# Cached index keys transposed during the opening, the sample indexer spread over the first late projection units, and attention's high halves made by GpSimd

## What is computed

```python
xn = rms_norm(x, norm1_g) * (1 + sc1) + sh1          # sc1, sh1 from silu(c) @ w_ada + b_ada
qa, ka, va, qb, kb, vb, iq, ik, iw = split_proj(xn @ w_in)
...
def indexer_scores(iq, iw, ik):                      # 8 heads of width 64
    dots = jnp.einsum('nqhd,nld->nqhl', iq, ik) * IDX_DIM ** -0.5
    return jnp.einsum('nqh,nqhl->nql', iw, jax.nn.relu(dots))
...
# sample: the index keys of the past come from paged memory
ik_all = concatenate([cache_idx_k[page_table].reshape(N, past, IDX_DIM), ik], axis=1)
sel, ok = select_keys(indexer_scores(iq, iw, ik_all), qpos, topk)
...
# mixer A (8 heads): three dilated windows, merged; mixer B (8 query heads, 2 key heads):
# softmax over the keys that the indexer chose
o = concatenate([oa, ob]); x = x + g1 * (o @ w_out)
x = x + g2 * ((silu(gate) * up) @ w_down)            # gate, up = xn2 @ w_gate_up
```

## Time and profile before

| what | value |
| --- | --- |
| device time, median of 3 runs (lowest to highest) | 1853.21 us (1852.08 to 1859.09) |
| profiled execution: its time, and its span | 1854.12 us, 1852.0 us |
| busy: PE, DVE, ACT, POOL | 1639.8, 872.8, 699.8, 551.4 us (89, 47, 38, 30% of the span) |
| HBM read, written | 115.29 MB, 27.04 MB (77 GB/s over the span) |

### The profile page before, as it was taken

How to read it: one execution, slowest core, us unless ns; L and a number is a source line. 1 busy time by engine, 2 the same in 40 slices (tenths; PEclk the granted TensorE clock), 3 DMA queues, 4 the chain that set the end, 5 groups by cost and what they waited for, 6 DMA issues and landing times.

```text
span 1852.0 us, 29649 instructions
## 1 busy us (share of the span) xinstructions
PE 1639.8 (89%) x10770; PEld 1520.8 (82%) x10770; DVE 872.8 (47%) x1992; ACT 699.8 (38%) x1812; POOL 551.4 (30%) x678
## 2 busy tenths in 40 slices
PE   5697779899857888886689889999999999999998
PEld 4594369899846776775379779999999999999998
DVE  2805687676856777786441443213213213213214
ACT  4415447756417878884131241111111111111111
POOL 0335146533643222211222042322322322322310
PEclk7799779999978999998889999999999999999999
DMA  7600015353333121101451121211211111211002
GB/s 243 242 24 13 5 44 164 107 179 99 96 88 125 58 92 40 60 1 56 158 196 35 46 68 35 58 45 34 57 45 34 57 45 33 58 45 28 18 1 94
DMA packets 138045, 135.30 MB, mean 73 GB/s; under 512 B 7229, under 2 KB 126957, under 8 KB 137302
## 3 DMA queue, kind: packets, MB, share of 16 engines
q1 hardware_dynamic: 136294, 131.07, 22.3%
q0 software_dynamic: 1648, 2.89, 0.5%
HBM read 115.29 MB, written 27.04 MB: 77 GB/s over the span
## 4 chain that ended last, share of the span: by engine, by line
PE 47%; DVE 2%; ACT 1%; DMA 1%; issue 0%; SPq 0%; DVEq 0%; ACTq 0%
PE bank L2284 27%; PE wide L2300 14%; PE bank L2263 5%; PE wide L2247 1%; DVE xn L2515 0%; DVE alo L2525 0%; DVE rstd L2499 0%; DMA out_y_p<-yn 0%; DMA ow<-in_w_out 0%; ACT ahi L2400 0%; DVE yn L2569 0%; ACT gwh L2358 0%; PE bank L2324 0%; ACT L2372 0%; ACT L2390 0%
## 5 line engine op out<-in xcount | busy, mean ns | idle before, releaser
L2536 DVE TENSOR_TENSOR hf<-bank,sg 128x352 f32<-128x352 f32 x66 | 34.7, 525 | 464.9 <-PE bank L2284 455.7
L2445 POOL TENSOR_TENSOR hlo<-hf,hhi 128x352 fp32r<-128x352 f32 x66 | 62.6, 949 | 505.2 <-ACT hhi L2374 505.2
L2284 PE MATMUL bank<-ahi,gwh 128*128 128x352 f32 x1056 | 196.3, 327 | 11.2 <-DVE hf L2536 6.6
L2549 DVE SCALAR_TENSOR_TENSOR x<-wide,modT,x 128x352 f32<-128x352 f32 (+1 forms) x264 | 151.3, 573 | 96.8 <-PE wide L2300 96.8
L2284 PE MATMUL bank<-alo,gwh 128*128 128x352 f32 x1056 | 192.7, 324 | 2.0 <-DVE alo L2525 2.0
L2284 PE MATMUL bank<-ahi,gwl 128*128 128x352 f32 x1056 | 194.2, 326 | 0.0
L2284 PEld LDWEIGHTS bank<-ahi,gwh 128*128 128x128 f32 x1056 | 176.2, 190 | 14.0 <-DVE hf L2536 6.9
L2284 PEld LDWEIGHTS bank<-alo,gwh 128*128 128x128 f32 x1056 | 174.9, 189 | 2.7 <-DVE alo L2525 2.7
L2284 PEld LDWEIGHTS bank<-ahi,gwl 128*128 128x128 f32 x1056 | 176.6, 191 | 0.0
L2300 PE MATMUL wide<-hlo,dwh 128*128 128x352 f32 x528 | 171.3, 324 | 0.0
L2300 PE MATMUL wide<-hhi,dwl 128*128 128x352 f32 x528 | 170.4, 323 | 0.0
(11 more groups left out here) (331 smaller groups left out, 3483.8 us busy)
## 6 DMA issues: line engine op xcount, KB each, us to landing
raw<-in_w_ada SPq DMA_DIRECT2D x24, 1024.0 KB, 7.7
gw<-in_w_gate_up SPq DMA_DIRECT2D x44, 512.0 KB, 5.0
raw<-in_w_in SPq DMA_DIRECT2D x11, 1024.0 KB, 5.8
dw<-in_w_down SPq DMA_DIRECT2D x22, 512.0 KB, 3.6
scr_x<-xT SPq DMA_DIRECT2D x1, 4224.0 KB, 17.7
xnat<-in_x_prompt SPq DMA_DIRECT2D x8, 512.0 KB, 5.6
scr_q<-ubuf SPq DMA_DIRECT2D x32, 128.0 KB
qn<-scr_q SPq DMA_DIRECT2D x8, 512.0 KB, 4.2
```

The source lines that it names most:

```text
L2284: mm = pe.matmul(pb[2 * s + side][:, 0:THIRD], a[r][:, k, side, :], b[:, k, third(th)], start=(p == 0 and k == 0), stop=(p == 2 and k == K ...
L2445: pool.tensor_tensor(hlo[:, r, third(th)], hf[:, (3 * r + th) % 2, :], hhi[:, r, third(th)].bitcast(F32), ALU.subtract).then_inc(h_lo, 1)
L2536: v.tensor_tensor(hf[:, s, :], pb[2 * s + 1][:, 0:THIRD], sg[:, s, :], ALU.mult).then_inc(h_mul, 1)
L2549: ins = v.scalar_tensor_tensor(out=x1[:, d, cols], in0=src[:, 0:n], scalar=modT[:, 40 + d, 0:1], in1=x1[:, d, cols], op0=ALU.mult, op1=ALU ...
```

## The change

1. **Pages in the opening.** POOL issues the 16 page loads right after the constants, ahead of its first weight split, no longer between the heads of the indexer. `START` gets two steps: PE transposes half of the pages into one wide bank (8 transposes), once after ada4 and once after ada6, and DVE copies each half with one instruction of 64x1024 elements into an `ikTs` that now holds all eight sequences. POOL's second weight split waits for the second of these transposes.
2. **Sample indexer spread.** Ahead of the late units PE keeps only the expansion and the nine small transposes. The score matmuls (8 of 64x256 and 8 of 64x32) follow late unit 0, their relu on ACT follows the same unit, the sums follow late unit 2, and DVE adds the row at slot 3. The search starts at slot 3, one step to a slot (73 over 73), and the tallies move by the same three. ACT no longer waits for the sums before the late stage, and POOL's split of the first late chunk no longer waits for the page transposes. `usq` becomes bf16, which makes room for rlS.
3. **High halves on POOL.** For heads 1 to 15 the rounding of qst, kst and vS moves from ACT to POOL (`tensor_copy`), with the waits that guard these buffers. POOL's list per head becomes q high, k high, q low, k low, v high, v low. Head 0 stays on ACT.

```diff
@@ -217,7 +217,8 @@
-    usq = T.at("usq", [P, 4, WCH], F32, T.end)
+    usq = T.at("usq", [P, 4, WCH], BF16, T.end)
+    rlS = T.at("rlS", [P, 2, NEWW], F32, T.end)
@@ -244,15 +245,15 @@
-    pg = T.at("pg", [P, NSEQ, 2, HD], F32, T.end)
...
+    pg = T.at("pg", [P, NSEQ, 2, HD], F32, WB + 24 * KD * P)
...
-    ikTs = T.at("ikTs", [HD, 2, NEWW], F32, UB)
-    rlS = T.at("rlS", [P, 2, NEWW], F32, T.end)
+    ikTs = T.at("ikTs", [HD, NSEQ, PAST], F32, S["pers"] - 36 * P * 2)
+    ikNew = T.at("ikNew", [HD, NSAMP], F32, T.end)
+    assert T.end <= S["pers"]
@@ -272,7 +273,7 @@
-        tallies_after.setdefault(slot_of(1 + 2 * q) + 1, []).append(q)
+        tallies_after.setdefault(slot_of(1 + 2 * q) + 4, []).append(q)
@@ -303,8 +304,9 @@
-    START = (["x0", "x1", "x2", "small", "x3", "x4", "ada0", "x5", "x6", "ada1", "x7", "x8", "ada2", "rs", "ada3"]
-             + [f"ada{a}" for a in range(4, ada_at)])
+    START = ["x0", "x1", "x2", "small", "x3", "x4", "ada0", "x5", "x6", "ada1", "x7", "x8", "ada2", "rs", "ada3",
+             "ada4", "pages0", "ada5", "ada6", "pages1", "ada7"]
+    AFTER_SAMPLE = 3
@@ -582,6 +584,7 @@
                 if order[n][0] == "ik":
+                    pe.wait_ge(sx_ev, 2)
@@ -619,6 +622,23 @@
                         ada_turn(turns[t])
+                    if u == NIDX:
+                        sample_scores()
+                    elif u == NIDX + 2:
+                        sample_sums()
+            def turn_pages(r):
+                pe.wait_ge(pg_in, 32 * NSEQ)
+                if r == 0:
+                    pe.wait_ge(x_lowT, NTILE + 1)
+                    pe.wait_ge(x_highT, NTILE + 1)
+                else:
+                    pe.wait_ge(sx_ev, 1)
+                for i in range(4):
+                    for j in range(2):
+                        mm = pe.transpose(wide[0][0:HD, PAST * i + j * P:PAST * i + (j + 1) * P], pg[:, 4 * r + i, j, :],
+                                          ident[:])
+                mm.then_inc(sx_tr, 1)
@@ -683,20 +703,22 @@
-                pe.wait_ge(sx_ev, 2)
+            def sample_scores():
+                pe.wait_ge(sx_ev, 4)
...
-                pe.wait_ge(pg_in, 32 * NSEQ)
-                for s in range(NSEQ):
-                    b = bank[2 + s % 2]
-                    if s >= 2:
-                        pe.wait_ge(sx_ev, s + 1)
-                    for j in range(2):
-                        mm = pe.transpose(b[0:HD, j * P:(j + 1) * P], pg[:, s, j, :], ident[:])
-                    mm.then_inc(sx_tr, 1)
-                    pe.wait_ge(sx_ev, s + 3)
-                    r = 32 * (s % 4)
-                    pe.matmul(wide[s // 4][r:r + 32, 0:NEWW], iqTs[:, s].rearrange("d h t -> d (h t)"),
-                              ikTs[:, s % 2, :], start=True, stop=True).then_inc(sx_mm, 1)
+                for g in range(2):
+                    for s4 in range(4):
+                        dst = wide[1][32 * s4:32 * s4 + 32, 512 * g:512 * g + NEWW]
+                        q = iqTs[:, 4 * g + s4].rearrange("d h t -> d (h t)")
+                        pe.matmul(dst[:, 0:PAST], q, ikTs[:, 4 * g + s4, :], start=True, stop=True)
+                    for s4 in range(4):
+                        dst = wide[1][32 * s4:32 * s4 + 32, 512 * g:512 * g + NEWW]
+                        q = iqTs[:, 4 * g + s4].rearrange("d h t -> d (h t)")
+                        mm = pe.matmul(dst[:, PAST:NEWW], q, ikNew[:], start=True, stop=True)
+                    mm.then_inc(sx_mm, 1)
+            def sample_sums():
@@ -710,6 +732,8 @@
+                elif step[:5] == "pages":
+                    turn_pages(int(step[5:]))
@@ -766,6 +790,8 @@
                     act.wait_ge(tr_fill, 4)
+                if c == 4:
+                    act.wait_ge(ix_acc, 48)
                 act.activation(whi[:, c % 2, :, 0:w], raw[:, n % 3, :, 0:w], ACT.Copy).then_inc(whi_done, 1)
@@ -887,13 +913,14 @@
-            for g in range(2):
-                act.wait_ge(sx_mm, 4 * (g + 1))
-                act.activation(rlS[:, g, :], wide[g][:, 0:NEWW], ACT.Relu).then_inc(sx_relu, 1)
+            def sample_relu():
+                for g in range(2):
+                    act.wait_ge(sx_mm, g + 1)
+                    act.activation(rlS[:, g, :], wide[1][:, 512 * g:512 * g + NEWW], ACT.Relu).then_inc(sx_relu, 1)
...
-            act.wait_ge(sx_sc, 1)
@@ -905,6 +932,8 @@
                         root(u - 1)
+                        if u == NIDX:
+                            sample_relu()
                         if turns:
@@ -970,8 +999,18 @@
+            def load_pages(s):
+                for j in range(2):
+                    page = pool.value_load(pages[0:1, 2 * s + j:2 * s + j + 1], min_val=0, max_val=n_pool - 1)
+                    pool.dma_start(pg[:, s, j, :],
+                                   A["cache_idx_k"][0, bass.ds(page, 1), :, :].rearrange("a p d -> (a p) d")
+                                   ).then_inc(pg_in, 16)
+            for s in range(NSEQ):
+                load_pages(s)
...
+            pool.wait_ge(sx_tr, 2)
@@ -986,23 +1025,14 @@
...
-                load_pages(h)
...
-            pool.wait_ge(sx_tr, NSEQ + 1)
@@ -1073,6 +1103,11 @@
+                elif step[:5] == "pages":
+                    r = int(step[5:])
+                    v.wait_ge(sx_tr, r + 1)
+                    v.tensor_copy(ikTs[:, 4 * r:4 * r + 4, :].rearrange("d s n -> d (s n)"), wide[0][0:HD, :]
+                                  ).then_inc(sx_ev, 1)
@@ -1145,11 +1180,10 @@
-            v.wait_ge(sx_tr, 1)
+            v.wait_ge(sx_tr, 3)
             v.tensor_copy(iqTs[:].rearrange("d n h t -> d h n t"),
                           bank[2][0:HD, 0:256].rearrange("d (h n t) -> d h n t", h=8, n=NSEQ))
-            v.tensor_copy(ikTs[:, 0, PAST:NEWW], bank[2][0:HD, 256:288])
-            v.tensor_copy(ikTs[:, 1, PAST:NEWW], bank[2][0:HD, 256:288]).then_inc(sx_ev, 1)
+            v.tensor_copy(ikNew[:], bank[2][0:HD, 256:288]).then_inc(sx_ev, 1)
             link(v.tensor_tensor(whead[:], bank[3][:, 0:16].rearrange("p (g h) -> p g h", g=2),
@@ -1159,14 +1193,11 @@
-            for s in range(NSEQ):
-                v.wait_ge(sx_tr, s + 2)
-                if s >= 2:
-                    v.wait_ge(sx_mm, s - 1)
-                v.tensor_copy(ikTs[:, s % 2, 0:PAST], bank[2 + s % 2][0:HD, 0:PAST]).then_inc(sx_ev, 1)
-            v.wait_ge(sx_sc, 1)
-            v.tensor_tensor(sco[0:NSAMP, ioff[6]:ioff[6] + NEWW], bank[2][0:NSAMP, 0:NEWW], valid[:],
-                            ALU.add).then_inc(ix_acc, 1)
+            def sample_row():
+                v.wait_ge(sx_sc, 1)
+                v.tensor_tensor(sco[0:NSAMP, ioff[6]:ioff[6] + NEWW], bank[2][0:NSAMP, 0:NEWW], valid[:],
+                                ALU.add).then_inc(ix_acc, 1)
@@ -1315,7 +1346,10 @@
-                        search(u - NIDX)
+                        if u - NIDX == AFTER_SAMPLE:
+                            sample_row()
+                        if u - NIDX >= AFTER_SAMPLE:
+                            search(u - NIDX - AFTER_SAMPLE)
@@ -1555,6 +1589,26 @@
+            def highs(h):
+                wait_q(pool, h)
+                pool.wait_ge(filled, head_fills[h - 1][-1] + 1)
+                pool.tensor_copy(qst[:, :, 0, :], qn[:, (h // 2) % 2, :, HD * (h % 2):HD * (h % 2) + HD]
+                                 ).then_inc(q_hi, 1)
+                if kbuild(h):
+                    r, cols = ksrc(h)
+                    wait_kv(pool, h)
+                    pool.tensor_copy(kst[:], kn[r][:, :, cols].unsqueeze(2).to_broadcast([P, NTILE, 2, HD])
+                                     ).then_inc(k_hi, 1)
+            def high_v(h):
+                if vbuild(h):
+                    hi, _ = halves(h)
+                    r, cols = ksrc(h)
+                    wait_kv(pool, h)
+                    if h >= 2:
+                        pool.wait_ge(o_mm, 2 * (h - 1))
+                    pool.tensor_copy(vS[:, h % 2, :, hi], vn[r][:, :, cols]).then_inc(v_hi, 1)
@@ -1575,7 +1629,9 @@
+                highs(h)
...
+                high_v(h)
@@ -1678,8 +1734,6 @@
-                if h >= 1:
-                    act.wait_ge(filled, head_fills[h - 1][-1] + 1)
@@ -1693,8 +1747,6 @@
-                    if h >= 2:
-                        act.wait_ge(o_mm, 2 * (h - 1))
@@ -1741,10 +1793,6 @@
-                if h + 1 < NH and i == 0:
-                    high(h + 1)
-                if h + 1 < NH and i == 7:
-                    high_v(h + 1)
```

11 lines of the change are left out of this document (2 added, 9 removed).

## The result

The changed kernel takes 1825.9 us (median of 4 executions, 1824.6 to 1827.7) against 1853.8 for the kernel before in the same comparison: ratio 0.9845, 95% interval 0.9823 to 0.9868, 28 us. Measured again with other kernels it gave 0.9857 (0.9837 to 0.9876). The forecast was 1836, the range 1823 to 1848: inside the range and in the forecast direction, but a gain 10 us larger than forecast, and near the time of the third rival (1824). The ratio is always the time over that of the kernel before in the same comparison. The profiled execution has a span of 1823.0 us against 1852.0, so 29.0 us have to be found.

The account below looks back on a forecast made before the run. PE was taken to bound the untouched output projection and feed-forward, so earlier savings count if they reach PE. Opening +1, sample indexer -8, attention -10.8 gave -17.8 us, 1854.1 to 1836.3, forecast 1836; range 1823 to 1848.

Parts of the forecast that it names:

- the third rival: Attention and late stage: ACT was the whole bound, 20 of 25.8 us arrive and the late stage gives 11; 1824, chance 0.13.
- The opening: Kernel start: added page loads, transposes and copies cost +1 us, between 0 and +6.
- The cover named for the copies: Opening: DVE's 4.63 us scaling beside POOL's weight split hides the page copies; without it they cost up to 3.4 us.
- The sample indexer: Between indexer and late units: earlier first late unit and search at slot 3 gain 8 us, between 0 and 11.7.
- the same score columns, 9.3 us: Late units: scores put back cost 9.3 us at the old rate; with sums of 2.13, taken at 6.8 us.
- keeps its length: Late stage, theory stated with the experiments: work begins when POOL's split is done, and the stage behind keeps its length.
- keeps its shape: Rest of the late stage: expected unchanged, the search having 73 steps over 73 slots instead of 73 over 76.
- Attention: Heads 1 to 15: taking roundings from ACT gains 10.8 us (9.6 plus 1.2, values nothing), between 0 and 25.8.
- POOL as supplier: Attention: POOL's copies cost 1.28 and 2.38 us like its subtraction, leaving 2.3 us to spare before PE wants the queries.
- The slower rival: Attention: POOL's copies come late, at twice the subtraction's cost, and PE waits at eight heads; 1867, chance 0.05.
- the search sets the late stage: Late stage: the search, starting no earlier than before, sets the pace and the late gain is 0; 1844, chance 0.15.
- Attention passes to DVE: Attention: DVE becomes the bound and the attention gain is lost; 1847, chance 0.12.

Follow-up runs that it names:

- one_row_group: Changed kernel with all eight sample score products written to PSUM partitions 0 to 31 instead of four groups of 32; 1829.5 us, ratio 0.9864.
- attn_only: Kernel before the change with only the changed attention function; 1838.3 us, ratio 0.9907.
- scores_first: Changed kernel with sample scores, relu and sums put back ahead of the late units and the search from slot 0; 1825.3 us, ratio 0.9832.
- prep_early: Changed kernel with scores, relu and sums ahead of the late units, search spacing kept, only its first two steps at slots 0 and 1; 1823.9 us, ratio 0.9836.
- highs_two_operands: Changed kernel with POOL's 35 high halves made by multiplication with ones instead of a copy; 1828.0 us, ratio 0.9867.
- prompt_prep: Changed kernel with the search's first-step prompt work at late unit 0, orientation following the row in slot 3, page copies on ACT; 1818.2 us, ratio 0.9815.

## Why the prediction was right, and where it was wrong

- **The opening**, +1 in the range 0 to +6: the traces differ by 2.7 at the last relu, the run without pages by 0.4 (traces) or 3.2 (medians). The size was in range. The cover named for the copies was only partly there: DVE's scaling still ran 4.62 us beside POOL's split, but began at 68.24 instead of 61.00, because the whole chain of modulations was later, and the split itself at 63.61 instead of 60.85. The rule for small rows of the Trainium skill, "DMA: Bandwidth & Descriptors", Specifications, by which the sum would have been 2 us more, can be neither seen nor excluded; the loads landed in 3.7 us (2.0 before), and POOL's queue had time for them.
- **The sample indexer**, -8: this is the term that was off most, measured -13.0 (-10.8 to -14.5 in the six other profiles with the change's layout, against the mean of the two with the old one). The step that failed is "the same score columns, 9.3 us", taken at 6.8 us together with the sums. Scores and sums cost 2.3 us. Of the 4.5 us less, `one_row_group` shows 2.9: four products at a time run side by side once nothing stands between them. The rest is what the higher clock and the lack of interruptions gave beyond the assumption (the sums took 1.16 us for 2.13). The sample row was done 14.0 us after the first late unit, not 18.9. The rest of the step held: from there to the wait's end was worked out as 29.6 us and measured as 28.5. With 2.3 in place of 6.8 us, 15 us of the 17.3 us of earlier start remained, and 13 arrived: the stage from its first late unit to the last norm scaling grew from 306.4 to 310.6 us, so the theory's "keeps its length" is good to a few microseconds only. That the rest of the stage "keeps its shape" was only near: at its end PE was 16.4 us ahead, but DVE's selection steps, 8.1 us ahead, held back the last scalings. The edit of `usq` to bfloat16, which the sum left out, did not change the price of ACT's squares (248 ns before, 255 after).
- **Attention**, -10.8: measured -15.3, repeated by `attn_only` (15.2). The mechanism was right, the sizes were small. A change of heads gave 1.2 to 1.3 us as assumed. Head 1, counted as nothing, gave with the change behind it 2.7 us up to the first value evacuation (21.3 and 18.6), of which about 1 us is the clock's later rise: with POOL's roundings and a late rise (`scores_first`, `prep_early`, `one_row_group`) it took 19.5 to 19.7; mixer B, counted at 2.4, gave 3.5 (716.5 to 859.5 before, 694.2 to 833.7 after). Values gave about 1, counted as nothing. And the sum had no term for the clock, whose fall at 682.5 cost 1.8 us before and is not there after.
- **POOL as supplier**: the copies took 0.61 and 1.04 us, at ACT's price and below the assumed one, as the rule on one-input work in the Trainium skill, "GPSIMD Engine Reference", 4.1 Engine selection, had it; the higher price was taken on purpose and, in `highs_two_operands`, made one wait of more than 0.2 us, at head 1. The slower rival needed copies of 4.4 us for keys; they took 1.04.
- **The rivals**: "the search sets the late stage" had the late gain at 0, and it was 13; the number is out, the mechanism is not. `scores_first` does not test it, since its earlier row and its three steps more cancel; at the stage's end DVE's selection steps, the last of the search, do hold the last scalings, and `prompt_prep`, with the prompt part of the search's first step moved ahead of the row, gained 3 to 5 us there. "Attention passes to DVE" is half true: PE now waits for pL alone, but that wait did not grow. The third rival had the right time, not the right reason: it took 20 us from attention and 11 from the late stage, where 15.3 and 13.0 came, and ACT was not the whole bound, since its value roundings gave a sixth of their 6.9 us. That its time was met is luck.

## What to carry to other kernels

Price a group of small matmuls by whether they can run together: rows of a stage in which each waits for a copy say nothing of what four cost back to back into four groups of output partitions. Before moving work off a busy engine, look what stands directly behind each piece: here 15.7 us came with 18.9 us of roundings that stood ahead of the next probabilities (some 3 of them through the matrix clock), and one from 6.9 us that did not. And when a late input is spread among other work, split the steps that wait for it: here the larger part of the search's first step did not need it.

## What the runs showed that was not expected

- DVE instructions of 32 columns took 4.58 us where they had taken 0.39, beside a weight split of POOL that began 0.1 us earlier; in the opening the scaling of 256 columns took 4.62 us in the same way.
- Four products of 64x256 for different groups of 32 output partitions took 0.64 us, for one group 1.91 us, with the same time of each record.
- POOL's copy of 128x512 took 0.61 us and of 128x1024 1.04 us, half of its two-operand instructions of the same shapes (1.28 and 2.38 us).
- A stretch that no edit touches, from attention's last value evacuation to the output projection, took 76.1 to 80.0 us from run to run, and the first projection moved by 3 us among equal openings. In the profile before, two groups of 16 value matmuls of the sample attention took 3.64 us each, in the one after 3.44 and then 1.92: the matrix clock rose from 1.2 to 2.4 GHz in one and not in the other. Differences of 3 us between two single traces are of that size.
- In attention the matrix clock fell to 1.2 GHz for 3.4 us, once or twice, in all three profiles in which ACT rounds queries and keys, and after its first 10 us in none of the eleven in which POOL does; each fall cost 1.5 to 1.8 us.
